# Dealing the first branch product out between the index scores of a hybrid attention/recurrent kernel

## The reference, cut to what matters

```
z = xn @ w_in
q, c_kv, q_idx, k_idx, w_idx, g_attn, x_rnn, g_rnn, merge = split_cols(z)
c_kv = rms_norm(c_kv, kv_norm_g)
s_idx = relu(einsum('btjd,bsd->btjs', q_idx, k_idx))      # 8 index heads of width 64
s_idx = einsum('btjs,btj->bts', s_idx, w_idx)             # weighted sum over the heads
_, idx = top_k(s_idx, topk)                               # the keys that attention uses
h = rg_lru(causal_depthwise_conv(x_rnn, conv_w, conv_b), w_rg_a, b_rg_a, ...)
y_rnn = (h * silu(g_rnn)) @ w_rnn_proj
gates = sigmoid(merge + b_merge)
```

## Time and profile before

| what | value |
|---|---|
| runs, median (lowest to highest) | 2155.19 us (2154.96 to 2160.63) |
| span of the profiled execution | 2155.7 us |
| PE busy | 2087.1 us, 97% of the span |
| DVE busy | 1519.0 us, 70% |
| ACT busy | 1022.8 us, 47% |
| POOL busy | 1006.8 us, 47% |
| mean granted TensorE clock | 0.988 |

### The profile page before, as it was taken

One profiled execution on the slowest core, in us unless ns is written; L12 is line 12 of the kernel. 1 busy time (PEld: TensorE's weight loads), 2 busy tenths in 40 slices (PEclk: granted clock), 3 DMA queues, 4 the chain that ended last, 5 costly groups with the idle time before them and its releaser, 6 DMA issues.

```text
span 2155.7 us, 31350 instructions
## 1 busy us (share of the span) xinstructions
PE 2087.1 (97%) x11601; PEld 1875.2 (87%) x11601; DVE 1519.0 (70%) x2879; ACT 1022.8 (47%) x1890; POOL 1006.8 (47%) x564
## 2 busy tenths in 40 slices
PE   8998999999999999999999999999999989999998
PEld 8845789999999999999999999999867767876677
DVE  4697558749998767878777888877688844017853
ACT  4366433358888743333333333334456642336632
POOL 2200255554446666665576666573435443430032
PEclk9998899999999999999999999999999999999999
DMA  5200124457778899999899999995312222220021
GB/s 195 69 11 1 50 88 144 163 182 262 253 260 293 323 338 333 332 341 353 318 337 343 344 323 357 326 336 181 108 59 88 73 84 103 94 79 1 1 78 60
DMA packets 142743, 414.10 MB, mean 192 GB/s; under 512 B 13184, under 2 KB 59904, under 8 KB 140800
## 3 DMA queue, kind: packets, MB, share of 16 engines
q1 hardware_dynamic: 105728, 277.86, 37.2%
q0 software_dynamic: 36864, 134.23, 16.7%
HBM read 370.62 MB, written 41.42 MB: 191 GB/s over the span
## 4 chain that ended last, share of the span: by engine, by line
PE 88%; DVE 5%; ACT 4%; issue 2%; DMA 0%; SPq 0%; DVEq 0%; ACTq 0%
PE bank L474 25%; PE bank L475 24%; PE bank L476 24%; PE bank L813 4%; DVE co L1798 2%; PE bank L992 2%; PE bank L1011 1%; PE wide L1011 1%; PE wide L494 1%; PE wide L1001 1%; DVE sidx L2273 0%; PE bank L1024 0%; PE wide L792 0%; DVE tmp L2308 0%; PE wide L501 0%
## 5 line engine op out<-in xcount | busy, mean ns | idle before, releaser
L2490 POOL TENSOR_TENSOR wl<-wraw,wh 128x1024 fp32r<-128x1024 f32 x273 | 685.7, 2515 | 814.3 <-ACT wh L1128 813.7
L474 PE MATMUL bank<-XH,wh 128*128 128x384 f32 (+2 forms) x1680 | 600.4, 357 | 13.9 <-issue 10.2
L475 PE MATMUL bank<-XL,wh 128*128 128x384 f32 (+2 forms) x1680 | 593.1, 353 | 0.0
L476 PE MATMUL bank<-XH,wl 128*128 128x384 f32 (+2 forms) x1680 | 589.2, 351 | 0.0
L1128 ACT CAST wh<-wraw 128x1024 fp32r<-128x1024 f32 x362 | 378.5, 1046 | 210.4 <-PE bank L476 190.4
L474 PEld LDWEIGHTS bank<-XH,wh 128*128 128x128 f32 x1680 | 317.6, 189 | 44.8 <-issue 19.7
L474 PE MATMUL bank<-WTH,wh 128*128 128x384 f32 x1024 | 347.4, 339 | 0.0
L476 PE MATMUL bank<-WTH,wl 128*128 128x384 f32 x1024 | 347.1, 339 | 0.0
L475 PE MATMUL bank<-WTL,wh 128*128 128x384 f32 x1024 | 346.8, 339 | 0.0
L475 PEld LDWEIGHTS bank<-XL,wh 128*128 128x128 f32 x1680 | 317.8, 189 | 23.8 <-issue 2.1
L476 PEld LDWEIGHTS bank<-XH,wl 128*128 128x128 f32 x1680 | 318.6, 190 | 22.1
(11 more groups left out here) (497 smaller groups left out, 3159.0 us busy)
## 6 DMA issues: line engine op xcount, KB each, us to landing
wraw<-in_wstream SPq DMA_DIRECT2D x362, 512.0 KB
g_scratch<-gs SPq DMA_DIRECT2D x12, 2048.0 KB, 7.4
gr<-g_scratch SPq DMA_DIRECT2D x15, 1536.0 KB
a_scratch<-tmp SPq DMA_DIRECT2D x72, 192.0 KB
tmp<-a_scratch SPq DMA_DIRECT2D x46, 192.0 KB
sq<-a_scratch SPq DMA_DIRECT2D x26, 192.0 KB
h<-in_hT SPq DMA_DIRECT2D x8, 264.0 KB, 6.6
fetched<-in_u_rows,diag POOLq DMA_INDIRECT x128
```

Of the source, the lines that this page charges most:

```text
L474: pe.matmul(o, w1, x1, start=n == 0, stop=False)
L475: pe.matmul(o, w1, x2, start=False, stop=False)
L476: m = pe.matmul(o, w2, x1, start=False, stop=n == len(ks) - 1)
L2490: return pool.tensor_tensor(lo, src, hi.bitcast(F32), ALU.subtract)
```

## The change

The first branch product `xr0` no longer stands as a block behind the scores. It becomes a generator, `first_branch`, and after each of the 24 scores TensorE issues one of its 24 passes. Its result goes to `halves[1]` and the transposed latent keys go to `halves[2]`, so neither takes a bank of the ring any more. The transposes and `branch_gates(0)` move behind the product `gr0`. On ScalarE the cast of one weight tile (`gr0`'s) moves from behind the relus to before the thirteenth, and the copy of the transposed latent keys moves behind the `lam` activations, before the copy of `xr1`.

```diff
-            bank = next_bank("ckv_t", (idx_out, ("ckv_t",)))
+            bank_of["ckv_t"] = bank = halves[2]
             pe.wait_ge(*idx_step.at("ckvn"))
...
+        def first_branch():
+
+            n = tile[0]
+            tile[0] += 1
+            bank_of["xr", 0] = bank = halves[1]
+            pe.wait_ge(*w_hi.at(n))
+            pe.wait_ge(*low_of(n))
+            for k in range(KT):
+                for sig, event in second_ready(k):
+                    pe.wait_ge(*sig.at(event))
+                w1, w2 = (w[n % NSPLIT][:, k * 128:k * 128 + 128] for w in (wh, wl))
+                pe.matmul(bank[:, :], w1, XH[:, k, 0:512], start=k == 0, stop=False)
+                yield
+                pe.matmul(bank[:, :], w1, XL[:, k, 0:512], start=False, stop=False)
+                yield
+                mm = pe.matmul(bank[:, :], w2, XH[:, k, 0:512], start=False, stop=k == KT - 1)
+                if k == KT - 1:
+                    mm.then_inc(*gemm.tell(("xr", 0), ("tile", n)))
+                yield
+
+        latent_steps, branch_steps = latent_keys(), first_branch()
...
                 pe.matmul(bank[:, 0:n], qi[p0:p0 + 64, j // 2, qt * 128:qt * 128 + 128], kx[p0:p0 + 64, 0:n],
                           start=True, stop=True).then_inc(*idx_mm.tell((j, qt)))
-
+                next(branch_steps)
...
+        for _ in branch_steps:
+            pass
         next(latent_steps)
         pe.wait_ge(*ld_rg.at("rg"))
-        product(XH, XL, *full(("xr", 0), (branch_x, 0)), x_ready=second_ready)
-        next(latent_steps)
         for c in range(8):
             if c + 1 < 8:
                 product(XH, XL, *full(("xr", c + 1), (branch_x, c + 1)))
-            branch_gates(c)
+            if c > 0:
+                branch_gates(c)
             product(XH, XL, *full(("gr", c), (silued, (c, 1))))
+            if c == 0:
+                next(latent_steps)
+                branch_gates(c)
...
             if n == 8:
                 roots("ckv", 512)
+            if n == 12:
+                stream()
...
-        stream()
         branch_in(0)
-        act.wait_ge(*idx_mm.at("ckv_t"))
-        act.copy(ckv[:, :, :],
-                 bank_of["ckv_t"][:, :].rearrange("p (j c) -> p j c", c=128)).then_inc(*idx_out.tell(("ckv_t",)))
         stream()
...
         act.activation(sps[:, 3, :], sps[:, 2, :], ACT.Ln).then_inc(*lam_act.tell("ln"))
+        act.wait_ge(*idx_mm.at("ckv_t"))
+        act.copy(ckv[:, :, :],
+                 bank_of["ckv_t"][:, :].rearrange("p (j c) -> p j c", c=128)).then_inc(*idx_out.tell(("ckv_t",)))
```

More of the change, by code:

```diff
@@ L894, in latent_keys, with second_ready @@
             yield
-        latent_steps = latent_keys()
+        def second_ready(k):
+            return (x_hi, ("two", k)), (x_lo_dve if k % 3 == 1 else x_lo_pool, ("two", k))
+        def first_branch():
[17 more added lines that the diff above has]
+        latent_steps, branch_steps = latent_keys(), first_branch()
         pe.wait_ge(*idx_out.at("kx2"))
@@ L916, in branch_gates @@
                       stop=True).then_inc(*branch_mm.tell((c, "i")))
-        def second_ready(k):
-            return (x_hi, ("two", k)), (x_lo_dve if k % 3 == 1 else x_lo_pool, ("two", k))
+        for _ in branch_steps:
+            pass
         next(latent_steps)
         pe.wait_ge(*ld_rg.at("rg"))
-        product(XH, XL, *full(("xr", 0), (branch_x, 0)), x_ready=second_ready)
-        next(latent_steps)
         for c in range(8):
```

## The result

The changed kernel took 2191.47 us (median of 4 runs, 2188.85 to 2192.39) against 2155.18 us for the kernel before beside it: ratio 1.0157, 95% interval 1.0141 to 1.0173. It is slower, as forecast, but by about 34 us and not by 16. The time lies outside the range. (The two medians are 36 us apart; the ratio and the two profiled executions give 34.) The profiled execution has a span of 2190.0 us against 2155.7, so 34.3 us are to be explained, at a mean granted clock of 0.977 against 0.988.

What follows compares the result with a forecast made beforehand. VectorE set the pace of the scores and a ring of waits that of the branch loop; dealt passes would make TensorE's index stage the bound. `mg1` ends 15.9 us later: 2155.2 + 15.9 = 2171.1 us, range 2159 to 2177.

Steps and rivals of the forecast that it cites:

- the mechanism at full clock: Index stage: lost score pairs, row changes and VectorE holds delay `mg1` by 15.9 us, carried on by the branch loop; chance 0.48.
- scores, passes and sums: TensorE in the index stage: 15.4 + 5.64 + 9.4 for row changes + 0.98 = 31.4 us from 1567.6.
- last sum done: VectorE's sum of the last score, held by GpSimd's low part for `gr0`, is done at 1601.85; before, 1588.43.
- second tiny operation done: Small VectorE operation behind the mask adds, for which ScalarE's Ln waits: ends at 1614.4, 15.8 us late.
- `mg0` starts, its wait: TensorE, ready at 1613.4, waits 2.2 us for ScalarE's copy of `xr1` to free the bank; `mg0` starts at 1615.6.
- `ix` done: VectorE's `ix`, at the end of its convolution work, ends at 1624.65; before, 1608.45.
- wait of `xr2`: TensorE before `xr2`: the new bank ring makes it wait 4 us for VectorE's `silued`, done at 1625.3.
- shift against before: End of `mg1`: 1644.0 against 1628.1 before, 15.9 us later, carried on by the branch loop.
- The second hold: VectorE's mask adds held by GpSimd's low part for `mg0`, directly behind the held last sum: +2.4 us.
- The 0.4 us added for later holds: VectorE up to `ix`: 0.4 us added because the later `xr1` copy moves GpSimd's two holds in the convolution.
- The rival with the clock falling in the new waits: Clock falls around TensorE's 2.2 and 4 us waits, costing at most 3.4 us: 2174.5 us; chance 0.09.
- The step that failed: TensorE's index-stage sum of 31.4 us from 1567.6, putting the last score at 1598.7 and `xr1` 9.8 us late.

Runs made afterwards that it cites:

- kernel with wide sums: Changed kernel with the latent keys' eight sums, still behind the sixth score, each over 128 columns of ones instead of one: 2173.09 us, ratio 1.0067.
- Pairs with the same one-column sums: Changed kernel with two passes behind each pair of scores instead of one behind each score: 2161.73 us, ratio 1.0018.
- single scores over 128 rows: Changed kernel with each index score taken over all 128 rows, so scores differ from the reference's: 2164.28 us, ratio 1.0032.
- block kernel: Changed kernel with the dealing undone: the first branch product runs as one block behind the scores again, the rest as changed: 2162.0 us, ratio 1.0015.
- the same order with other gate banks: First branch product as a block behind the scores, rest as changed, plus block 0's two gate banks taken ahead of `gr0`: 2158.77 us, ratio 1.0006.
- fours: Changed kernel with four passes behind each four scores, and two top-k rounds moved into later blocks: 2154.14 us against 2157.76, ratio 0.9982.
- a gap of 1.04 us: Changed kernel with its sums behind the last score, and TensorE made to wait for VectorE's sixth sum in their old place: 2190.54 us, ratio 1.0143.

## Why the prediction was half right

**The direction and the mechanism at full clock were right, step by step.** The kernel with wide sums is the changed kernel at 2.4 GHz in the score stage, so it tests the forecast's own sum. Its VectorE and TensorE rows:

```profile
1599.16 2.42 DVE L2301 SCALAR_TENSOR_TENSOR sidx<-rb,wx,sidx 128x512 f32<-128x512 f32 x1 [0.73 <-ACT rb L1556]
1601.51 2.89 DVE L2306 TENSOR_TENSOR sidx<-sidx,cst 128x128 f32<-128x128 f32 x3
...
1613.79 0.16 DVE L2345 TENSOR_SCALAR sps<-sps 128x8 f32<-128x8 f32 x1
...
1620.70 2.85 DVE L2373 TENSOR_TENSOR tmp<-rt,tmp 128x512 f32<-128x512 f32 x1
```

```profile
1615.30 0.47 PE L474 MATMUL bank<-XH,wh 128*128 128x512 f32 x1 [2.19 <-ACT rs L1564]
...
1624.29 0.47 PE L474 MATMUL bank<-XH,wh 128*128 128x512 f32 x1 [3.19 <-DVE rt L2376]
```

| step | forecast | kernel with wide sums |
|---|---|---|
| scores, passes and sums | 31.4 us | 1598.76 - 1567.52 = 31.24 |
| last sum done | 1601.85 | 1601.58 |
| second tiny operation done | 1614.4 | 1613.95 |
| `mg0` starts, its wait | 1615.6, 2.2 us | 1615.30, 2.19 us |
| `ix` done | 1624.65 | 1623.55 |
| wait of `xr2` | 4 us | 3.19 us |
| shift against before | +15.9 us | +16.3 (distance), +14.5 (ratio 1.0067) |

The second hold was real: the mask adds took 2.89 us, directly behind a held sum. So was the new wait for `silued`. The 0.4 us added for later holds was too much: from the second tiny operation to `ix` are 9.60 us, not 10.26. VectorE was already 0.45 us ahead at that operation, so `ix` came 1.1 us earlier than forecast. The rival with the clock falling in the new waits was partly true as well. From 1625 to 1630 the granted clock was 0.66, and `xr2` took 7.21 us (1624.29 to the gates at 1631.50) instead of 5.64. One error is 1.1 us too much, the other 1.6 too little; that the shift comes out within half a microsecond is luck.

**The step that failed** is "So TensorE needs 15.4 + 5.64 + 9.4 + 0.98 (the sums between, 1570.21 to 1571.19) = 31.4 us from 1567.6". It was worked out from rows that all stood at 2.4 GHz, and took for granted, without a reason, that the new stage would keep that clock. The terms themselves were right, as the 31.24 us with wide sums show, but in the changed kernel the stage measured 1615.97 - 1567.64 = 48.33 us, 38.24 of them at 1.2 GHz. The account then is:

- +16.3 us from the mechanism forecast (wide sums against before, 84.19 - 67.87), with the 1.6 us of slow clock in `xr2` in it;
- +16.8 us from the clock in the score stage (101.01 - 84.19). The stage itself lost 17.2; part of that came out of the wait of `mg0`, which was 0.65 us in the changed kernel and 2.19 with wide sums;
- 34.3 - 33.1 = 1.2 us elsewhere in the program, not traced further.

The distances are from one execution each. By the ratios the two parts are 14.5 and 19.4 us, so each is known to some 2 to 3 us.

The prediction had a rival for the clock, but put it where TensorE waits, and bounded it at 3.4 us with the earlier trace rows. No rival let it fall in a stage in which TensorE never waits. The trace of before had warned of nothing in this place: the same sums there are followed by several scores together. What it did show was that I had made the stream thinner: 24 scores and passes took 31 us where the scores and the block had taken less than 23 (1567.63 to 1590.23, with the waits between them), and rows at 2.4 GHz cannot say whether the clock survives that.

The Trainium skill (TensorE: Matmul & The Clock Gate, "HAM oscillation — how this bites in real kernels") gives as its abstract rule that TensorE must have no long idle gaps. By that rule this stage was safe: its busy time was 10.00 of 10 us and the sums are matmuls. The trace disagrees, with a granted clock of 0.50 in each of the three windows from 1580 to 1610.

**What stays open.** No run gives the amount of work at which the clock falls or rises. Pairs with the same one-column sums kept it, and so did single scores over 128 rows; single scores over 64 rows did not. These differ in both time per pass and rows used, and the runs do not separate the two. Nor do they show why the block kernel had 0.92 and 0.91 on the mean in its score windows where the same order with other gate banks had 1.00. TensorE waits for the same relu in both, 1.44 and 1.45 us, and for 1.43 us in the kernel before, which kept 1.00 too. So among scores in pairs a longer gap than the 1.04 us above left the clock alone in two of these kernels and not in the third.

## What to carry to other kernels

When passes are dealt out between small matmuls, keep those that run beside each other together. Pairs instead of singles brought the loss from 33 us down to 4; with fours, and with two top-k rounds taken out of the way, the same idea gained some 4 us. Price every stage that gets thinner at both levels of the clock, and read the granted clock of the new stage before anything else, since a stage at half clock looks like a fully busy engine with no waits. Look inside such a stage for the one place where hardly anything is streamed, be it a short wait or a row of one-column matmuls, and move it out or widen it.

## What the runs showed of the hardware that I had not expected

- About a microsecond with little streamed tipped the granted clock from 1.00 to 0.50 in a thin alternation: eight one-column matmuls in 0.95 us, or a gap of 1.04 us. It did not come back in the 38 us that the alternation went on. It was back soon after the products began (1617.54; the passes are 0.23 us apart again from 1618.84).
- The same eight matmuls with 128 columns each take 1.05 us instead of 0.95 and hold the clock. Widening these eight was worth 16.8 us.
- A score over 64 rows between two passes costs 0.38 to 0.40 us more than one over 128 rows, the same at all three widths. So the extra goes with the change of rows and not with the columns.
